# Modulation columns of six feature tiles read in pairs, in rows of 1 KB, and x turned token-wise ahead of the keyed matmuls

## The reference, cut to what matters

```python
mod = split(silu(c) @ ada_w + ada_b, 6)            # c: 1024 values, ada_w: 1024 x 6144
a   = rmsnorm(x, g_pre) * (1 + mod[1]) + mod[0]    # scale and shift, one value for each feature
b_gate, c_gate, v = split(a @ w_in, 3)             # the short gated convolution follows
h   = x + mod[2] * rmsnorm(gated_conv(...) @ w_out, g_post)
```

## Time and profile before

| | |
|---|---|
| median of 3 runs | 753.81 us (753.56 to 754.33) |
| time of the profiled execution | 753.58 us |
| its span | 751.9 us |
| TensorE busy | 739.8 us, 98% of the span |
| DVE / ACT busy | 74% / 49% |
| the opening stage, first L1477 | from 0 to 65.45 us |

### The profile page before, as it was taken

The page is one execution under the profiler, slowest core; times in us unless marked ns, Lnnn a source line. Parts: engine busy times, 40 slices in busy tenths (PEclk is TensorE's granted clock), DMA queues, the critical chain, the costliest instruction groups (busy, mean ns, idle before and its releaser), DMA issues.

```text
span 751.9 us, 13218 instructions
## 1 busy us (share of the span) xinstructions
PE 739.8 (98%) x5328; PEld 687.6 (91%) x5328; DVE 556.9 (74%) x805; ACT 365.7 (49%) x455; POOL 12.1 (2%) x29
## 2 busy tenths in 40 slices
PE   6999999999999999999999999999999999999998
PEld 6789965999998888899979999999999999999998
DVE  5667998865656843489899976859779988887441
ACT  4116332655455333496555456584557554554330
POOL 0000000000000000020000001000000000000000
PEclk9999999999999999999999999999999999999999
DMA  9999998365556976536444252337453555443640
GB/s 285 305 324 388 382 362 316 118 228 198 184 168 197 350 236 202 207 137 224 169 169 168 93 188 99 125 129 266 171 222 121 215 186 199 156 134 129 206 138 29
DMA packets 61903, 152.69 MB, mean 203 GB/s; under 512 B 3040, under 2 KB 42336, under 8 KB 51616
## 3 DMA queue, kind: packets, MB, share of 16 engines
q1 hardware_dynamic: 61024, 149.43, 58.7%
q0 software_dynamic: 544, 1.84, 0.7%
q10 hardware_dynamic: 288, 0.76, 0.3%
HBM read 150.97 MB, written 1.05 MB: 202 GB/s over the span
## 4 chain that ended last, share of the span: by engine, by line
PE 86%; DVE 9%; ACT 2%; DMA 2%; issue 1%; SPq 0%; ACTq 0%; DVEq 0%
PE ps L1479 19%; PE ps L1478 19%; PE ps L1477 19%; PE ps L1633 4%; PE ps L1634 4%; PE ps L1632 4%; PE ps L1679 4%; PE ps L1554 4%; DVE w_lo L911 3%; DVE cacc L1251 2%; ACT w_hi L543 1%; PE ps L1803 1%; PE ps L1801 1%; PE ps L1802 1%; DMA keyed_even<-in_w_sc_in 1%
## 5 line engine op out<-in xcount | busy, mean ns | idle before, releaser
L911 DVE TENSOR_TENSOR w_lo<-raw,w_hi 128x2048 fp32r<-128x2048 f32 (+2 forms) x116 | 245.9, 2122 | 85.1 <-ACT w_hi L543 84.9
L1477 PE MATMUL ps<-a_hi,w_hi 128*128 128x256 f32 x1024 | 290.4, 284 | 0.0
L1479 PE MATMUL ps<-a_hi,w_lo 128*128 128x256 f32 x1024 | 289.5, 283 | 0.0
L1478 PE MATMUL ps<-a_lo,w_hi 128*128 128x256 f32 x1024 | 288.0, 281 | 0.0
L543 ACT ACTIVATE w_hi<-raw 128x2048 fp32r<-128x2048 f32 (+2 forms) x116 | 205.9, 1778 | 98.1 <-PE ps L1634 47.4
L1477 PEld LDWEIGHTS ps<-a_hi,w_hi 128*128 128x128 f32 x1024 | 193.2, 189 | 1.3 <-issue 0.7
L1478 PEld LDWEIGHTS ps<-a_lo,w_hi 128*128 128x128 f32 x1024 | 193.5, 189 | 0.6 <-issue 0.5
L1479 PEld LDWEIGHTS ps<-a_hi,w_lo 128*128 128x128 f32 x1024 | 191.8, 187 | 0.0
L1477 PE MATMUL ps<-up_hi,w_hi 128*128 128x256 f32 x192 | 54.6, 284 | 0.0
L1479 PE MATMUL ps<-up_hi,w_lo 128*128 128x256 f32 x192 | 54.3, 283 | 0.0
L1478 PE MATMUL ps<-up_lo,w_hi 128*128 128x256 f32 x192 | 53.8, 280 | 0.0
(11 more groups left out here) (279 smaller groups left out, 957.4 us busy)
## 6 DMA issues: line engine op xcount, KB each, us to landing
raw<-in_w_z_in SPq DMA_DIRECT2D x26, 1024.0 KB, 4.8
raw<-in_w_up SPq DMA_DIRECT2D x22, 1024.0 KB, 4.7
raw<-in_w_mlp_in SPq DMA_DIRECT2D x16, 1024.0 KB, 5.0
raw<-in_w_mlp_out SPq DMA_DIRECT2D x16, 1024.0 KB, 5.9
raw<-in_w_down SPq DMA_DIRECT2D x16, 704.0 KB, 4.2
raw<-in_ada SPq DMA_DIRECT2D x32, 256.0 KB, 6.4
raw<-in_ada_half SPq DMA_DIRECT2D x8, 1024.0 KB, 7.6
raw<-in_ada SPq DMA_DIRECT2D x8, 1024.0 KB, 7.2
```

The costliest lines, as they stand in the source:

```text
L911: e.tensor_tensor(w_lo[:, slot, 0:words], raw[:, unit_slot, 0:words], w_hi[:, slot, 0:words].bitcast(f32), SUB).then_inc(raw_used, 1)
L1477: e.matmul(dst, w_hi[:, slot, cols], hi, start=start, stop=False, skip_group_check=skip)
L1478: e.matmul(dst, w_hi[:, slot, cols], lo, start=False, stop=False, skip_group_check=skip)
L1479: return e.matmul(dst, w_lo[:, slot, cols], hi, start=False, stop=stop, skip_group_check=skip)
```

## The change

Five edits, all in the opening stage.

1. **Pairs.** Tiles 0 and 1 are read as before. Tiles 2 to 7 are read by `pair_part(u)`: unit u = 2q + v holds the scale (v = 0) or the shift (v = 1) columns of both tiles of pair q, two transfers of 512 KB in rows of 256 words (1 KB). Each pair is the same 2 MB as before, in 4 transfers in place of 8. `pair_sum(q, v)` sums a unit with eight instructions of 256 words.
2. **The sums' order.** Both sums of a pair must be there before the first tile's columns: `tile_columns(t)` waits for `raw_used` of `t // 2 * 2 + 2`. Sums live in `ada_acc[:, 0, :]` (`pair_acc`).
3. **c alone.** c's 8 columns of `params` come in a transfer of their own, first on ACT's queue; the other 458 columns (`par_in`) are waited for later. silu(c) stands ahead of the squares.
4. **Squares unadded.** DVE's two additions are gone; TensorE sums eight blocks of squares in place of four.
5. **Turning.** TensorE has 8 `keep_busy` matmuls ahead of x, turns x's second half (8 matmuls, banks 2 and 3) behind the sum of squares and ahead of the keys, and ACT copies it in one instruction behind tile 0's high part. `turn_x` and its two copies are gone; `keep_busy(2)` is gone, `keep_busy(5)` is 4.

```diff
+            def pair_part(u):
+                if u >= RAW_SLOTS:
+                    e.wait_ge(raw_used, u - RAW_SLOTS + 1)
+                for i in range(2):
+                    e.dma_start(raw[:, u % RAW_SLOTS, i * D:(i + 1) * D].rearrange("p (j f) -> p j f", j=4),
+                                ada[u % 2 * 4:u % 2 * 4 + 4].rearrange("j p (i f) -> i p j f", i=2)[i][:, :, u // 2 * 256:u // 2 * 256 + 256])\
+                     .then_inc(part_in[u], 16)
...
-                part(2 * q)
-                part(2 * q + 1)
+                pair_part(2 * q)
+                pair_part(2 * q + 1)
...
+            def pair_sum(q, v):
+                u = 2 * q + v
+                e.wait_ge(part_in[u], 32)
+                if u:
+                    e.wait_ge(raw_used, u)
+                acc = pair_acc[:, q % 2, v, :]
+                src = raw[:, u % RAW_SLOTS, :].rearrange("p (i j f) -> p i j f", i=2, j=4)
+                ch.link(e.tensor_scalar(acc, src[:, 0, 0, :], silu_c[:, 0:1], None, MUL))
+                for k in range(1, DT - 1):
+                    ch.link(ada_part(src[:, k % 2, k // 2, :], silu_c[:, k:k + 1], acc))
+                ada_part(src[:, 1, 3, :], silu_c[:, 7:8], acc).then_inc(raw_used, 1)
...
-            for t in range(1, DT):
-                tile_sum(t)
+            second_tile_sum()
+            columns(1)
+            pair_sum(1, 0)
+            pair_sum(1, 1)
+            for t in range(2, DT):
                 if t == DT - 1:
                     a_low(0, 6)
                 columns(t)
+                if t < DT - 2:
+                    pair_sum(t // 2 + 1, t % 2)
...
+            keep_busy(8)
             e.wait_ge(x_landed[0], 16)
...
                 if t:
-                    e.wait_ge(raw_used, t + 1)
+                    e.wait_ge(raw_used, t // 2 * 2 + 2)
                     e.wait_ge(cols_ready, t)
```

More of the change, by code:

```diff
@@ L620, in token_chain @@
                         between()
+            e.dma_start(par[:, 0:8], params[:, 0:8]).then_inc(c_in_cols, 16)
             e.dma_start(x[:, 4:8, :], x_in[:, 4:8, :]).then_inc(x_landed[1], 16)
[L624 removed]
+            e.dma_start(par[:, 8:N_PARAMS], params[:, 8:N_PARAMS]).then_inc(par_in, 16)
+            e.wait_ge(c_in_cols, 16)
+            e.wait_ge(const_set, 1)
+            e.activation(silu_c[:, :], pcol("c", 0, 8), ACT.Silu).then_inc(c_ready, 1)
             e.wait_ge(x_landed[0], 16)
             e.activation(x_tok[:, 0, 0:512], flat(x[:, 0:2, :]), ACT.Square).then_inc(x_sq, 1)
[L627 to L629 removed]
             e.wait_ge(x_landed[1], 16)
@@ L659, in _ @@
                 a_high(t)
+                if t == 0:
+                    e.wait_ge(tile_turned, 2)
+                    e.activation(x_tok[:, :, 512:1024], ps[:, 2:4, :], ACT.Copy).then_inc(x_tok_in, 1)
                 if t == 6:
-                    x_by_token(2)
                     high_at(0)
-            x_by_token(3)
             def sc_copy(grp):
@@ L1068, in _ @@
             e.wait_ge(x_landed[0], 16)
[L1069 to L1073, removed]
-            e.wait_ge(x_landed[1], 16)
[L1075 to L1079, removed]
+            two = flat(x[:, 2:4, :])
+            e.tensor_tensor(x_tok[:, 1, 0:512], two, two, MUL).then_inc(x_stat_in, 1)
+            e.wait_ge(x_landed[1], 16)
+            two = flat(x[:, 6:8, :])
+            e.tensor_tensor(x_tok[:, 1, 512:1024], two, two, MUL).then_inc(x_stat_in, 1)
             e.wait_ge(c_ready, 1)
@@ L1083, in _ @@
             scale_x(0, 2)
+            e.wait_ge(par_in, 16)
             columns(0)
@@ L1500, in mod_sums, with keep_busy @@
                     mod_sum(vector, acc, i, bank)
+            def keep_busy(n):
+                for _ in range(n):
+                    e.matmul(ps[:, 5, 0:P], ident[:, :], ones[:, :], start=True, stop=True)
             e.wait_ge(const_set, 3)
+            keep_busy(8)
             e.wait_ge(x_landed[0], 16)
@@ L1507, in _ @@
             mm.then_inc(tile_turned, 1)
+            e.wait_ge(x_sq, 1)
             for h in range(2):
                 e.wait_ge(x_stat_in, h + 1)
-                for i in range(2):
-                    mm = e.matmul(ps[:, 6, 0:T], ones[:, :], x_tok[:, 0, h * 512 + i * T:h * 512 + (i + 1) * T],
-                                  start=h == 0 and i == 0, stop=h == 1 and i == 1)
-            mm.then_inc(x_stat, 1)
+                if h:
+                    e.wait_ge(x_sq, 2)
+                for engine in range(2):
+                    for i in range(2):
+                        at = h * 512 + i * T
+                        mm = e.matmul(ps[:, 6, 0:T], ones[:, :], x_tok[:, engine, at:at + T],
+                                      start=h + engine + i == 0, stop=h + engine + i == 3)
+            mm.then_inc(x_stat, 1)
+            e.wait_ge(x_landed[1], 16)
+            for c in range(2):
+                for i in range(4):
+                    mm = e.matmul(ps[:, 2 + c, i * P:(i + 1) * P], x[:, 4 + i, c * P:(c + 1) * P], ident[:, :], start=True, stop=True)
+            mm.then_inc(tile_turned, 1)
             def tile_columns(t):
                 if t:
-                    e.wait_ge(raw_used, t + 1)
+                    e.wait_ge(raw_used, t // 2 * 2 + 2)
                     e.wait_ge(cols_ready, t)
+                else:
+                    e.wait_ge(first_scale, 1)
                 for v in range(2):
@@ L1523, in tile_columns @@
                         continue
-                    if t == 0:
-                        e.wait_ge(first_scale, 1)
-                    mm = e.matmul(dst, tile_acc[:, t % 2, v, :], ones[:, 0:1], start=True, stop=True)
+                    mm = e.matmul(dst, pair_acc[:, t // 2 % 2, v, t % 2 * P:(t % 2 + 1) * P], ones[:, 0:1], start=True, stop=True)
                 mm.then_inc(part_ps, 1)
@@ L1535, in first_tile_shift @@
                     e.matmul(ps[:, 7, 0:1], src[:, k % 2, k // 2, :], silu_c[:, k:k + 1], start=k == 0, stop=k == DT - 1)
[L1537 to L1545, removed]
             def by_key(k, grp):
@@ L1555, in by_key @@
                 return mm
[L1557 to L1561, removed]
             first_tile_shift()
             tile_columns(0)
-            keep_busy(5)
+            keep_busy(4)
             e.wait_ge(x_tok_in, 1)
@@ L1570, in _ @@
                         e.wait_ge(key_in[k // 2][grp // 2], 16)
+                    if k == 0 and grp == 2:
+                        e.wait_ge(x_tok_in, 2)
                     mm = by_key(k, grp)
```

28 lines of the change are left out of this document (10 added, 18 removed).

## The result

| | before | changed |
|---|---|---|
| median | 753.88 us (753.26 to 754.33, 6 runs) | 757.71 us (755.60 to 758.28, 6 runs) |
| ratio, 95% interval | | 1.0052 [1.0042, 1.0063] |
| profiled execution, its span | 753.58, 751.9 us | 757.62, 755.9 us |
| mean granted clock of the profiled execution | 0.999 | 0.993 |
| next stage (first L1477, now L1496) begins | 65.45 us | 69.44 us |

The change makes the kernel slower by 0.5%, 3.8 us. The span is 4.0 us longer, and so is the opening stage (69.44 − 65.45): everything is in the first 70 us, which is where to look.

A forecast was written before the change was run, and what follows sets the result against it. TensorE, busy 98% of the span, was taken as the bound. Terms: +3.1 us by tile 2, +0.2 for pair 2's landing, −0.9 for waits, −1.8 for four turns, giving 754.5 us; range 752.9 to 756.7.

The forecast's parts named there:

- The front: Up to tile 0's columns: turning to columns takes 8.9 us, so these columns come 1.05 us later.
- The order of the sums: Ahead of tile 2: two sums in a row, 8.0 us, idle TensorE 3.3 us; tile 2 starts 3.1 us later.
- Pair 2's landing: Ahead of tile 3: pair 2's scales land at 33.0, so tile 3 starts at 38.2, adding 0.2 us.
- The width: Transfers of the pairs: 1 KB rows save 0.65 us for each MB, 2.0 us by pair 2's scales.
- Tiles 3 to 7: Rest of the opening stage: tiles start 5.7 us apart without waits, the last takes 5.1 us.
- The likeliest case: Whole kernel: time within 752.3 to 755.3 us counts as same, chance 0.70; forecast 754.5 us, next stage at 66.1.
- the forecast course: Opening stage with the clock held: next stage starts at 66.1, 0.65 us later, giving 754.5 us; chance 0.70.
- the fall of the clock: Rival, gap ahead of tile 2: clock drops to 1.2 GHz, 2.2 us lost, 756.7 us; chance 0.17.
- upper bound: Same course with the clock rising later in the front: 1.5 us more, stage ends at 67.4, 755.8 us.

The follow-up runs named there:

- e11: e7 with 10 matmuls whose result nobody reads in its gap ahead of tile 2's columns; 754.28 us, ratio 1.0014.
- e4: Changed kernel with the pairs taken back (narrow rows, one sum a tile), keeping c alone, squares unadded and turning; 752.71 us, ratio 0.9989.
- e1: Changed kernel with 14 matmuls whose result nobody reads in the gap ahead of tile 2's columns; 755.04 us, ratio 1.0023.
- e9: e1 with each unit of a pair read in four transfers with 512 B rows in place of two with 1 KB rows; 757.37 us, ratio 1.005.
- e5: Kernel before with only the pairs and the sums' order added, keeping its own front and turning; 756.35 us, ratio 1.004.
- e3: Changed kernel with both the 14 unread matmuls in the gap and keep_busy(7) in place of keep_busy(4) behind tile 0's columns; 755.09 us, ratio 1.0022.
- e7: Changed kernel with wide rows for all pairs kept, but sums made tile by tile over both units of a pair; 756.45 us, ratio 1.0041.
- e2: Changed kernel with keep_busy(7) in place of keep_busy(4) behind tile 0's columns; 757.57 us, ratio 1.0051.
- e8: e4 with wide rows for tiles 4 to 7 only, summed tile by tile over both units of a pair; 756.57 us, ratio 1.0043.
- e12: e4 with DVE's two additions of squares put back, so TensorE sums four blocks of squares; 753.31 us, ratio 1.0.
- e10: Changed kernel with the turning of x's second half moved from the front into the gap ahead of tile 2's columns; 754.96 us, ratio 1.0021.

## Why the prediction was wrong

I forecast 754.5 us in 752.9 to 756.7, with "same" likeliest; it is 757.7, slower. Point by point:

- **The front**: right. First columns at 14.72 (14.83 forecast), second sum at 17.32 (17.4). By the spacing of its records, TensorE was at the fast pace from 6.4 us on, 4.5 after the first `keep_busy` (4.4 forecast); the view of the granted clock doesn't show this first rise and gives 1.00 from the start. From the start of the turning to the columns it was 9.2 us (8.9), since half pace took 0.5 us from the turning and not 0.2; x had landed 0.4 us sooner, which made up for it. That the forecast is met to 0.1 us is in part luck: in the ten profiled runs with this front, the turning took from 2.05 us (e11) to 3.18 (e4), by where the pace rose, and the first columns came from 14.23 to 15.44.
- **The order of the sums**: right. Two sums of 8.1 us (8.0), a wait of 3.2 us (3.3). The columns of tile 1 came 0.6 later than forecast, behind a front fall that I hadn't foreseen and that costs next to nothing in the end.
- **Pair 2's landing**: mis-sized. Forecast 33.0, it is 33.7 to 33.8, and tile 3's bias in e1 is 38.2, where I had the later start of the tile's matmuls. The width was nearly right (e9 to e1: 1.8 us; I took 2.0, and the two rates give 1.9, since they are 0.62 us for each MB and not 0.65). The rest is the queue, which runs late from the front on: with narrow rows and the new front the same columns land at 35.59 (e9) in place of 34.93. In the changed kernel SP issues the second half of the first keys at 12.14; in the kernel before it did so at 11.27. e5, with wide rows and the old front, bears this out: pair 2's scales land at 33.24, so some 0.5 us of the miss belong to the front. Which of the front's edits delays the queue wasn't tried.
- **Tiles 3 to 7**: right, 5.70 us each and 5.1 for the last.
- **The likeliest case as a whole**: with the clock held it would be e1 or e3, 755.04 and 755.09, stage end 66.75 (66.1 forecast). It lacks the 0.7 us of the landing and no more.
- **The step that failed** is the sentence that the forecast course has 0.70 and the fall of the clock 0.17: the wait took the clock down. The prediction says that no row shows such a fall, and it also says that a gap of 3.3 us is new to this kernel; to give the fall only 0.17 was to read the absence of rows as evidence. The rival's own text had the right mechanism, and its price was short: 2.2 us by a return 4.4 us after work resumed, where TensorE worked at half pace for 5.9 us (31.23 to 37.15) and lost 2.7. It was also added to the forecast course's 66.1 and not to its upper bound, so that two small misses, 0.5 and 0.7, carried the result over the edge at 756.7.

In terms, each from two runs: the front −0.9 us (e4 against the kernel before, 753.61); the order of the sums +4.7 (e9 against e4); wide rows −2.3 (e1 against e9); the clock +2.7 (changed against e1). Together 757.7, as they must, since each starts where the last ends. How well each is known shows in two other ways of taking it: the stage ends give −1.3, +5.0, −2.3 and +2.7, the ratios −0.8, +4.6, −2.0 and +2.2. The order's 4.7 us is its price in narrow rows: there tile 2's bias is 4.1 us later than in e4 (33.13 against 29.03) and tile 3's 5.3 (40.01 against 34.72), since DVE sums pair 2's scales, once they have landed, ahead of tile 3's columns. Wide rows give 2.3 us of it back.

The Trainium skill, "TensorE: Matmul & The Clock Gate", section "HAM oscillation", warns that waits between bursts of matmuls put the array back to its lower rate. The trace agrees with the warning, 0.50 from inside the gap on, though the gap of 3.2 us is a shorter wait than the section calls harmful, and e7 falls after 2.3 us. I should have let the warning weigh more than a missing row. In "DMA: Bandwidth & Descriptors", section "Why small descriptors are slow (HBM only)", the Trainium skill gives about three cycles on top of each packet's beats, an estimated 8% less time for 1 KB rows. The runs show more: of 34 to 44 us, e9 moved 315 GB/s with about half of its bytes in 512 B rows, e1 348 with all in 1 KB rows; if those run at 348 in both, the short rows ran at an estimated 286, near the 290 of the earlier trace rows, which is 18% less time for the wide ones.

What stays open: why the half pace lasted 6.8 us in the changed kernel and in e2, but 3.4 in e5, e7 and e8; and what decides whether the clock falls in the front. It isn't the kernel alone: e4's profiled run keeps its clock, but six of e4's eleven timed runs have a mean clock of 0.998, and so has e1's profiled run, with the front's fall alone. One of e1's ten runs and two of e11's eleven took 1.6 and 1.9 us longer than the median; no trace shows why.

## What to carry to other kernels

Merging transfers ties what they feed: count what the first consumer must now wait for, and put it against the queue's time saved; here 4.7 us against 2.3. And a new idle stretch of the engine that bounds the kernel costs its length and then the clock: where nobody has measured a gap of that length in the kernel, a fall belongs into the likely cases, and a few unread matmuls in it show in one run what the clock's part is.

## What the runs showed of the hardware that I had not expected

- Single idle stretches of 2.3 us (e7), 2.5 us (e8), 3.2 us (e5, changed) and 3.8 us (e2) brought the granted clock to 0.5, in the changed kernel 0.9 us before work resumed, in e5 1.6 us after (work from 29.8, half pace from 31.4). 1.1 us (before), 1.2 us (e11, e12), 1.7 us (e10, ahead of 18.97) and 0.7 and 1.0 us close together (e10) didn't.
- The clock can fall without an idle stretch of that length. At 16.7 us it went to 0.5 behind one-column matmuls, unread ones and an idle half microsecond. With three unread matmuls more it stayed up (e2, e3; all eleven timed runs of e3 have a mean clock of 1.0), but in the profiled runs of e4 and e12 it stayed up without them, as in five of e4's eleven timed runs, which have a mean of 1.0.
- How much a fall costs depends on what else is late: 1.7 us of lost pace cost some 0.5 us in e5 (0.2 to 0.6 by its timed runs), behind a landing, and all of it in e7.
- After the same 16 records of `keep_busy`, begun at 1.9 us, TensorE reached its fast pace at different times: before 5.4 us in e10 and e11, near 6.4 in the changed kernel, near 8.0 in e4. No edit explains it.
